# Down projection of a hybrid decoder layer: 18 of 22 halves as seven products of quarter sums

## The reference

```python
h = rmsnorm(x, pre_ffn_g[l])
up = causal_depthwise_conv(h @ w_up[l], conv_w[l], conv_b[l])   # width 2 x 5632, 3 taps
gate, val = jnp.split(up, 2, axis=-1)
y = (jax.nn.gelu(gate, approximate=True) * val) @ w_down[l]      # 5632 -> 2048
x = x + rmsnorm(y, post_ffn_g[l])
```

## Time and profile before

| | |
|---|---|
| runs (device us) | 2618.12, 2616.05, 2616.42; median 2616.42 |
| profiled execution, its own time | 2616.87 us |
| its span | 2615.1 us |
| mean granted TensorE clock | 0.999 |
| loop of 20 halves in the span | about 1318 to 2563 us |
| DMA | 372.03 MB, mean 142 GB/s |

### The profile page before, as it was taken

How to read it: one execution, slowest core, us unless ns; L and a number is a source line. 1 busy time by engine, 2 the same in 40 slices (tenths; PEclk the granted TensorE clock), 3 DMA queues, 4 the chain that set the end, 5 groups by cost and what they waited for, 6 DMA issues and landing times.

```text
span 2615.1 us, 44288 instructions
## 1 busy us (share of the span) xinstructions
PE 2598.0 (99%) x18036; PEld 2433.3 (93%) x18036; DVE 1890.7 (72%) x2673; ACT 1145.9 (44%) x1540; POOL 197.1 (8%) x273
## 2 busy tenths in 40 slices
PE   9999999999999999999999999999999999999998
PEld 8999999999999888888999999999999999999997
DVE  7897888788878545336787667677676767677777
ACT  8543434443444322234454444444444444444443
POOL 0100000000000100000001111111111111111111
PEclk9999999999999999999999999999999999999999
DMA  6434343343343833434236555555555555555567
GB/s 243 142 120 138 114 141 112 115 126 118 105 153 119 327 130 129 152 129 153 81 112 143 138 140 134 134 138 137 137 130 138 135 132 137 135 132 144 130 147 271
DMA packets 107659, 372.03 MB, mean 142 GB/s; under 512 B 12448, under 2 KB 12448, under 8 KB 101584
## 3 DMA queue, kind: packets, MB, share of 16 engines
q1 hardware_dynamic: 72864, 264.28, 31.6%
q0 software_dynamic: 34608, 105.06, 18.2%
HBM read 297.98 MB, written 67.11 MB: 140 GB/s over the span
## 4 chain that ended last, share of the span: by engine, by line
PE 95%; DVE 3%; issue 1%; DMA 0%; ACT 0%; DVEq 0%; SPq 0%; ACTq 0%
PE ps L643 31%; PE ps L645 31%; PE ps L644 31%; PE ps L735 1%; PE ps L682 1%; PE ps L725 1%; DMA w_raw<-in_w 0%; PE ps L709 0%; DVE w_hl L1643 0%; DVE big L2101 0%; DVE w_hl L1636 0%; DVE w_hl L2042 0%; DVE h_lo L2206 0%; DVE mixing L1697 0%; DVE w_hl L2036 0%
## 5 line engine op out<-in xcount | busy, mean ns | idle before, releaser
L643 PE MATMUL ps<-h_hi,w_hl 128*128 128x256 f32 (+1 forms) x2032 | 611.8, 301 | 4.1 <-DVE w_hl L2042 2.2
L645 PE MATMUL ps<-h_hi,w_hl 128*128 128x256 f32 (+1 forms) x2032 | 605.5, 298 | 0.0
L644 PE MATMUL ps<-h_lo,w_hl 128*128 128x256 f32 (+1 forms) x2032 | 605.4, 298 | 0.0
L643 PE MATMUL ps<-w_hl,h_hi 128*128 128x512 f32 (+1 forms) x1168 | 433.6, 371 | 2.8 <-DVE w_hl L1643 2.2
L644 PE MATMUL ps<-w_hl,h_hi 128*128 128x512 f32 (+1 forms) x1168 | 429.4, 368 | 0.0
L645 PE MATMUL ps<-w_hl,h_lo 128*128 128x512 f32 (+1 forms) x1168 | 429.1, 367 | 0.0
L643 PEld LDWEIGHTS ps<-h_hi,w_hl 128*128 128x128 f32 x2032 | 388.6, 191 | 19.9 <-DVE w_hl L1643 3.3
L644 PEld LDWEIGHTS ps<-h_lo,w_hl 128*128 128x128 f32 x2032 | 388.6, 191 | 13.3 <-issue 1.0
L645 PEld LDWEIGHTS ps<-h_hi,w_hl 128*128 128x128 f32 x2032 | 388.5, 191 | 11.4
L1093 ACT ACTIVATE w_hl<-w_raw 128x768 fp32r<-128x768 f32 x152 | 128.6, 846 | 446.8 <-PE ps L645 446.7
L1349 ACT ACTIVATE w_hl<-w_raw 128x768 fp32r<-128x768 f32 x168 | 142.1, 846 | 405.1 <-PE ps L645 405.1
(11 more groups left out here) (272 smaller groups left out, 5636.0 us busy)
## 6 DMA issues: line engine op xcount, KB each, us to landing
w_raw<-in_w SPq DMA_DIRECT2D x487, 512.0 KB, 3.5
y_scratch<-work POOLq DMA_DIRECT2D x160, 256.0 KB, 6.0
gate_scratch<-mixing POOLq DMA_DIRECT2D x8, 1024.0 KB, 6.8
mixing<-in_x POOLq DMA_DIRECT2D x4, 1024.0 KB, 6.9
mixing<-mixing POOLq DMA_DIRECT2D x16, 256.0 KB, 3.5
merged<-gate_scratch POOLq DMA_DIRECT2D x4, 1024.0 KB, 14.9
g_ret<-gate_scratch POOLq DMA_DIRECT2D x4, 1024.0 KB, 13.9
y_scratch<-work POOLq DMA_DIRECT2D x8, 512.0 KB, 20.9
```

Source lines behind the costliest of these rows:

```text
L643: pe.matmul(bank, s_hi, m_hi_, start=first, stop=False, skip_group_check=skip)
L644: pe.matmul(bank, s_hi, m_lo_, start=False, stop=False, skip_group_check=skip)
L645: return pe.matmul(bank, s_lo, m_hi_, start=False, stop=last, skip_group_check=skip)
```

## The change

18 of the 22 half down projections (groups 0 to 8, done in halves g = 1 to 9) use the same seven-product scheme as the up stage. The other four (the loop's last two halves, and the last group behind the loop) stay plain.

- TensorE (`down_quads`): two column blocks (sub) of 512 columns, each two chunks; per chunk 7 products x 2 token blocks x 3 passes with 256 moving columns, that is 168 matmuls per half in place of 96.
- The weight stream's down chunks are stored as quarters, and go through the same rounds as up chunks: sums, two casts, two subtractions, for all 12 chunks of a half. The recombination of the up products is split around round 9 (`u_early` ahead of the raw split, `u_last` behind the sums' split).
- The activations need quarter sums as well: once per group, at rounds 5 to 7 of the first half, three tiles are split, four dependent additions make the forms (`make_forms`), three more are split (10 VectorE instructions and 6 of ScalarE, in place of 4 and 4).
- Gate taps, val taps, gelus and products move out of the down stage into rounds 2, 3 and 4 of the next half's up stage.
- Each of the seven products leaves its bank on its own: 14 leaves and 14 accumulates per half in place of 8, into y7 in HBM (4 column blocks x 7 products x 256 KB). There are seven staging tiles; two of them are the halves of gbuf, which gate linear writes too, so it waits for their accumulates. The first group (g = 1) stores without accumulating, and the clearing of y goes.
- `sum_products` recombines the seven sums at the end, for each pair of column blocks: POOL reads products into staging tiles and adds them to others in HBM, 14 accumulates a time, in steps with waits; ScalarE's first leave of the next half waits for all of them.
- The two plain halves add into the recombined quarters; y is read back in 16 pieces of 256 KB.
- POOL's descriptor space is set to 2048 bytes per partition (it stood at its default), and the room goes to the new tiles.

```diff
+QUAD_HALVES = HALVES - 2
+QUAD_GROUPS = QUAD_HALVES // 2
+SUB = 2
+STAGES = 7
...
+SUB_BANKS = ((7, P1, Q6, P2, Q7, Q4, Q3), (Q5, 7, P1, Q6, P2, Q7, Q4))
+LEAVE = ((0, 1, 2, 3, 4, 5, 6), (0, 2, 3, 4, 5, 6, 1))
+AFTER_SUBS = (Q3, Q5, P1, Q6, P2, Q7, Q4)
...
+def stage(n):
+
+    first = left_before(QUAD_HALVES)
+    return n % STAGES if n < first else 2 + (n - first) % (STAGES - 2)
...
-        staged = [part(1024 + t * NB, NB) for t in range(TT)]
+        staged = [gbuf[:, 0, :], gbuf[:, 1, :]] + [part(1024 + t * NB, NB) for t in range(TT)] +                  [at("staged_6", -2, [NB])[:, :]]
+        f1_hi, f1_lo = at("f1_hi", -14, [2, S], F32R), at("f1_lo", -10, [2, S], F32R)
+        s4_hi, s4_lo = at("s4_hi", -6, [2, HB], F32R), at("s4_lo", -4, [2, HB], F32R)
...
-            pool.memset(zeros, 0.0).then_inc(zeros_set, 1)
-            pool.wait_ge(zeros_set, 1)
-            for t in range(TT):
-                for c in range(2):
-                    pool.dma_start(y_dram[t, :, c * 1024:c * 1024 + 1024], zeros).then_inc(y_cleared, 16)
-            pool.wait_ge(y_cleared, 16 * 2 * TT)
...
+            def added(n):
+
+                for slot in range(STAGES):
+                    pool.wait_ge(y_added[slot], 16 * stage_uses(n, slot))
+
+            def accumulate_products(g, e):
+
+                for sub in range(SUB):
+                    for j, k in enumerate(LEAVE[sub]):
+                        n = left_before(half_index(g, e)) + 7 * sub + j
+                        pool.wait_ge(y_left, n + 1)
+                        target = y7_dram[SUB * e + sub, ORDER[k]]
+                        if g == 1:
+                            pool.dma_start(target, staged[stage(n)]).then_inc(y_added[stage(n)], 16)
+                        else:
+                            pool.dma_start(target, staged[stage(n)], accum_op=ALU.add)\
+                                .then_inc(y_added[stage(n)], 16)
...
+            def sum_products(e):
+
+                a, b = SUB * e, SUB * e + 1
...
+                        pool.dma_start(x[d][j], y7_dram[d, p]).then_inc(product_back, 16)
+
+                def add(j, p):
+                    for d in (a, b):
+                        pool.dma_start(y7_dram[d, p], x[d][j], accum_op=ALU.add).then_inc(product_moved, 16)
+
+                added(left_before(QUAD_HALVES - 1 + e))
+                fetch(0, P1)
+                fetch(1, Q5)
+                pool.wait_ge(product_back, fetched + 64)
+                add(0, Q6)
+                add(0, C11)
+                add(1, C12)
+                pool.wait_ge(product_moved, moved + 96)
+                fetch(0, Q6)
+                pool.wait_ge(product_back, fetched + 96)
+                add(0, C22)
+                add(0, C12)
+                pool.wait_ge(product_moved, moved + 160)
+                fetch(0, C22)
+                pool.wait_ge(product_back, fetched + 128)
+                add(1, C22)
+                add(0, C21)
...
+            for g in range(1, QUAD_GROUPS + 1):
+                for e in range(2):
+                    accumulate_products(g, e)
+                    if (g, e) == (QUAD_GROUPS, 0):
+                        sum_products(0)
+            sum_products(1)
+            for dd in range(2):
+                accumulate_plain(0, dd)
...
+            def down_quads(c, s, w, act_count):
+
+                pe.wait_ge(act_lo, act_count)
+                e, left = s * 7 - 7, left_before(w)
+                waits = (((y_left, left), (p1_left, s), (u_step, e + 1), (u_step, e + 2), (u_step, e + 3),
+                          (u_step, e + 4), (u_step, e + 5)),
+                         ((u_step, e + 7),) + tuple((y_left, left + k) for k in range(1, 7)))
+                for sub in range(SUB):
+                    for i in range(SUB):
+                        pe.wait_ge(lo_ready, c + SUB * sub + i + 1)
+                        w_h, w_l = quad_split(i)
+                        for k, p in enumerate(ORDER):
+                            if i == 0 and (waits[sub][k][0] is not y_left or waits[sub][k][1]):
+                                pe.wait_ge(*waits[sub][k])
+                            bank, col = ps[SUB_BANKS[sub][k]], slice(COLUMN[p] * HB, COLUMN[p] * HB + HB)
+                            o_h, o_l = down_operand(p, i)
+                            for m in range(2):
+                                tok = slice(m * P, m * P + P)
+                                mm = passes(bank[:, m * HB:m * HB + HB], (o_h[:, tok], o_l[:, tok]),
+                                            (w_h[:, col], w_l[:, col]), i == 0 and m == 0, i == SUB - 1, True)
+                            if i == SUB - 1 and k < 6:
+                                mm.then_inc(y_done, 1)
+                        mm.then_inc(chunk_used, 1)
...
+                if g:
+                    for slot in range(2):
+                        uses = stage_uses(left_before(half_index(g, e) + 1), slot)
+                        act.wait_ge(y_added[slot], 16 * uses)
...
+            def leave(n, bank, scale=1.0):
+
+                if stage_uses(n, stage(n)):
+                    act.wait_ge(y_added[stage(n)], 16 * stage_uses(n, stage(n)))
+                for e in range(2):
+                    if n == left_before(QUAD_HALVES - 1 + e):
+                        act.wait_ge(product_moved, moved_seen + 16 * 14 * (e + 1))
+                act.activation(staged[stage(n)], bank, ACT.Copy, scale=scale).then_inc(y_left, 1)
+
+            def leave_product(g, e, sub, j):
+
+                w, k = half_index(g, e), LEAVE[sub][j]
+                if k < 6:
+                    act.wait_ge(y_done, done_before(w) + 6 * sub + k + 1)
+                else:
+                    act.wait_ge(chunk_used, half_chunk_0(g, e) + KH + SUB * sub + SUB)
+                if sub == 0 and j == 0:
+                    act.wait_ge(prod_ready, 2 * (2 * g + e))
+                leave(left_before(w) + 7 * sub + j, ps[SUB_BANKS[sub][k]][:, :], -1.0 if ORDER[k] in (Q4, Q5) else 1.0)
...
+            def first_forms_hi(g, free):
+
+                act.wait_ge(chunk_used, free)
+                for a, src, c in ((0, 0, slice(0, HB)), (2, 1, slice(0, HB)), (4, 1, slice(HB, S))):
+                    act.wait_ge(prod_ready, 4 * g + 2 + 2 * src)
+                    act.activation(late_pieces(a)[0], vbufs[src][:, :, c], ACT.Copy).then_inc(act_hi, 1)
+
+            def second_forms_hi(g):
+
+                act.wait_ge(forms_made, 4 * g + 1)
+                act.activation(late_pieces(6)[0], vbufs[1][:, :, HB:], ACT.Copy).then_inc(act_hi, 1)
+                act.wait_ge(forms_made, 4 * g + 3)
+                act.activation(f1_hi[:, :, :], vbufs[0], ACT.Copy).then_inc(act_hi, 1)
+                act.wait_ge(forms_made, 4 * g + 4)
+                act.activation(s4_hi[:, :, :], vbufs[1][:, :, 0:HB], ACT.Copy).then_inc(act_hi, 1)
 
 
...
+            def quad_half(g, e, tasks):
+
+                c, n, s = half_chunk_0(g, e), sums_before(g, e), 2 * g + e
+                tasks = {**tasks, **conv_tasks(s - 1), KH: lambda: leave_p1(s),
+                         KH + 2: lambda: [leave_product(g, e, 0, j) for j in range(5)],
+                         KH + 3: lambda: [leave_product(g, e, 0, j) for j in (5, 6)],
+                         KH + 4: lambda: [leave_product(g, e, 1, j) for j in range(3)],
+                         KH + 5: lambda: [leave_product(g, e, 1, j) for j in range(3, 7)]}
+                for i in range(2, PER_HALF + 2):
+                    quad_hi(c, i, c + (i - 1))
+                    quad_sum_hi(n + i, i)
+                    if i in tasks:
+                        tasks[i]()
...
+            def quad_round(c, n, i, ahead=None, between=(None, None)):
+
+                ahead = i + 1 < KH if ahead is None else ahead
+                if between[0]:
+                    between[0]()
+                if ahead and not between[1]:
                     quad_sum_one(c, n + 1, i + 1)
                 raw_lo_of(c, i)
-                if ahead:
+                if ahead and not between[1]:
                     quad_sum_two(n + 1, i + 1)
                 sums_lo_of(n, i)
+                if between[1]:
+                    between[1]()
+                    quad_sum_one(c, n + 1, i + 1)
+                    quad_sum_two(n + 1, i + 1)
                 if ahead:
                     quad_sum_three(n + 1, i + 1)
...
+            def make_forms(g):
+
+                (a11, a21), (a12, a22) = ((v[:, :, 0:HB], v[:, :, HB:]) for v in vbufs)
+                m = 4 * g
+                dve.wait_ge(act_lo, splits_before(g) + 3)
+                TTm(a22, a21, a22, ALU.add).then_inc(forms_made, 1)
+                dve.wait_ge(forms_made, m + 1)
+                TTm(a21, a11, a21, ALU.subtract).then_inc(forms_made, 1)
+                dve.wait_ge(forms_made, m + 2)
+                TTm(a11, a22, a11, ALU.subtract).then_inc(forms_made, 1)
+                dve.wait_ge(forms_made, m + 3)
```

(36 more changed lines are left out.)

253 lines of the change are left out of this document (153 added, 100 removed).

## The result

The changed kernel takes **2694.8 us** (median of four runs, 2691.8 to 2697.1) against 2617.0 for the kernel before: ratio 1.0296, interval 1.0284 to 1.0308. That is 78 us slower where 117 were forecast. The profiled execution has a span of 2695.4 us, 80.3 more than before (its own time is 2697.1).

The account below looks back on a forecast made before the run. The prediction took TensorE, busy 99% of the span, to bound the kernel. It summed 2616.9 - 28.8 (TensorE) + 36.8 (VectorE) + 80 (DMA) + 28 (recombination) + 1 (tail) to 2734 us, range 2618 to 2820.

Parts of the forecast that it names:

- TensorE: Down stage of 18 halves: 168 narrower matmuls take 20.16 us instead of 21.76, 1.60 less each, 28.8 in all.
- VectorE: Its lag in the rounds stalls TensorE 3.65 us per first half and 0.43 per second, 36.8 us in all.
- usable spare of 1.33 us: Lag VectorE may build up behind its steady beat in chunk rounds before TensorE stands; 1.65 less 0.32 for late chunks.
- Those very rows test this: Claim that two 2.64 us tap tasks in the earlier trace confirm the lag rule: stall 0.43 worked out, 0.44 seen.
- DMA lateness: Accumulates in a burst make gate linear, and some leaves, late: 5.0 us in each of 16 halves, 80 us.
- 9 x 1.75 + 3.5 x 1.65 = 21.5 us of work: DMA engines' work up to the ninth accumulate, from 51.2 to 73.0 us, 5.6 late for gate linear.
- price of 1.75: Time in us one 256 KB accumulate was taken to cost the 16 DMA engines, from readings of 1.72 and 1.90.
- Signs named for the lateness: Right: accumulates landing after 10 us or more; wrong: under 9 us, and TensorE idle under 1.6 us per half.
- Recombination: sum_products, run twice near the end, holds ScalarE's next leave: 14 us each, 28 us, ends 0 and 40.
- ScalarE is held 13 to 22 us: Wait of its first leave after sum_products: six dependent steps of 62 to 71 us against 49 available.
- The tail: Reading y in 16 pieces instead of 6 after all accumulates: +1 us, ends 0 and 6.
- Rival 1: DMA engines keep up and only VectorE's lag counts: 2625 to 2640 us, chance 0.17.

Follow-up runs that it names:

- small_forms: Changed kernel with the forms made on 16 of 256 columns from the second group on, the rest of each form left out: 2664.7 us.
- casts_later: Changed kernel with ScalarE's three casts of forms moved behind its casts of chunk 7: 2686.3 us.
- taps_spread: Changed kernel with val taps in round 4 and products in round 6 of second halves, instead of 3 and 4: 2691.3 us.
- plain_stores: Changed kernel with all product transfers of the loop as plain stores instead of accumulates, sums over groups left out: 2651.1 us.
- gate_early: Changed kernel with gate linear waiting for a half's first two accumulates only, the other twelve leaves sharing five tiles: 2729.2 us.
- no_sum: Changed kernel without the recombination of the seven sums in HBM, both times, and without ScalarE's wait for it: 2658.1 us.
- before_small_space: Kernel before with only POOL's descriptor space set to 2048 bytes per partition: 2619.0 us, ratio 1.0003.
- all_off: Changed kernel with plain stores, no recombination in HBM and forms on 16 of 256 columns from the second group on: 2598.6 us.

## Why the prediction was right, and where it was not

- **TensorE.** Right: a down stage of 20.15 us with TensorE never idle (2071.35 to 2091.50), 1.6 less than 21.76.
- **VectorE.** Right, and nearly to the tenth: 0.44 and 3.69 us a half against 0.43 and 3.65, 37.2 against 36.8. The single gaps are 0.34, 1.55, 0.53, 0.30 and 0.53 at chunks 4, 7, 8, 9, 10, and some 0.1 more is lost behind each, as the next matmul comes late; 0.43, 1.6, 0.57, 0.43 and 0.62 were worked out. small_forms, casts_later and taps_spread took out the parts of it named. The step that carried this was the usable spare of 1.33 us, read from two tasks in the earlier trace rows. "Those very rows test this" claims too much: the 1.33 was worked out from the same late cast (5.48 for 5.04 us) as the 0.44 it was tested on. The test is the changed kernel.
- **DMA lateness.** The mechanism holds (plain_stores), the size is off by a factor of 2.7: 0.8 to 2.6 us in a first half and 1.0 to 2.9 in a second where 5.0 were charged. The step that was mis-sized is "9 x 1.75 + 3.5 x 1.65 = 21.5 us of work". The prices measured are 1.44 and 1.39, and the queues overlap by 10%: (9 x 1.44 + 3.5 x 1.39) / 1.10 = 16.2. By that the ninth accumulate would land at 67.4 us, just when gate linear was due; measured, the side of gate linear costs 1.3 us a half (17.7 over 14 halves) where 4.7 were charged. The price of 1.75 came from stretches of the kernel before in which an accumulate's packets took longer, 1.72 and 1.90 us per 256 KB against 1.44 in a denser burst: the share of 99% over 3 us was read as capacity. Why packets take longer there stays open.
- **The tiles.** A second fault lies in the same part. ScalarE waited in the leaves, and TensorE for banks in chunk 0 (0.3 to 1.5 us in most halves from the fifth on, 0.7 in the mean), priced at 0.3, and chunk 0 was not among the chunks named; gate_early shows how sensitive this side is.
- **Signs named for the lateness.** The landing time (10.6 us at the median) was as forecast, and idle time of TensorE, 1.4 us and more in each half from the 4th on, was 4.1 in the mean, over the 1.6 us named as the bound.
- **Recombination.** Mechanism right, size low: 41.6 by the table, above even my upper end of 40, and 36.7 by removal (no_sum), against 28. The steps' own length was right at its lower end (61.9 us against 62 to 71). "ScalarE is held 13 to 22 us" held too (19.95), but TensorE lost nearly all of it, not 14, and then ran at half clock.
- **The other edits.** The tail cost nothing (-1.2 behind the loop), and the descriptor space nothing with eight accumulates a half (before_small_space). The clearing of y was not tried by itself; the part ahead of the loop, in which it stood, took 1.3 us more in this run, less than it varies by between runs.
- Rival 1 (the DMA engines keep up) fell: with its 2625 to 2640 it needed plain_stores' kind of transfer. The Trainium skill, page "DMA: Bandwidth & Descriptors", section "Anatomy of one DMA", gave by its fit an estimate of 0.6 us of data for 256 KB; the plain stores come near it (0.70), the accumulates with 1.44 do not, and without that difference (plain_stores) the 30 us are gone.

The forecast of 2734 was too high by 39 against the median, 37 against the profiled execution: +50 in one term, -14 in another. That the total came nearer to the mark than its largest term is in part luck: the two errors have opposite signs.

## What to carry to other kernels

Count what a cheaper algorithm adds on the other engines against the gain per stage before anything else: here 1.6 us a half were bought with 2.1 us a half of VectorE's lag (mean of 0.44 and 3.69), although VectorE's mean load was under 80%. How much an engine can hide is read from a place where two tasks already follow each other, not from its busy share. No engine's first task of a stage should wait for a chain of dependent DMAs: from HBM to HBM, without borrowed tiles, the same recombination cost TensorE nothing.

## What the runs showed of the hardware that was not expected

- An accumulating DMA to HBM costs the 16 engines 1.44 us per 256 KB in a dense burst (2 KB rows, from a tile) and 1.30 to 1.43 from HBM in 8 KB rows, but 1.72 to 1.90 in the sparser stretches of the kernel before; a plain store costs 0.70. A load of 512 KB costs 1.39 beside accumulates and 1.63 alone; beside plain stores it costs 39.4% x 20 / (2.11 / 0.524) = 1.96 (plain_stores, 2061 to 2081 us). These are prices of a stretch, not constants.
- Within each hole of TensorE (17.4 and 18.7 us) the granted clock fell to 0.50, and it stayed there through the first matmuls behind the hole, 27 and 21 in the rows above. The Trainium skill, page "TensorE: Matmul & The Clock Gate", section "What's actually happening", has the clock of an idle TensorE at half; the trace agrees. The cost is small: of the 20.2 us in the 18th half 17.9 are gaps, the other 2.3 are slow matmuls.
- POOL's issue of an accumulate took 1216 ns at the median and up to 2222 in the changed kernel, 849 before, and 540 for a plain store. The small descriptor space alone does not do it (before_small_space); whether it does with fourteen transfers queued was not tried. It weighs little: POOL is 12% busy and has 2% of the chain.
- With accumulates the runs of one kernel differ by more (2655 to 2667 us in no_sum) than with plain stores, where they agree within 3 us, and in all_off within 0.2.
